# w_ada times silu(c) accumulated by VectorE and summed by matmuls with ones, in place of split matmuls

## What is computed

```
mod = jax.nn.silu(c) @ w_ada + b_ada            # [1, 3072]
shift, scale, gate = jnp.split(mod[:, None, :], 3, axis=-1)
h = rms_norm(x, norm_g) * (1 + scale) + shift
z = h @ w_in
...                                             # MLA attention and MoBA attention on z
return x + gate * y
```

## Time and profile before

| | us |
|---|---|
| median of 3 runs (1778.47 to 1781.76) | 1781.65 |
| profiled execution | 1779.26 |
| its span, first to last instruction | 1777.2 |
| PE busy in the span | 1680.2 |
| VectorE busy | 1063.4 |
| ScalarE busy | 902.1 |
| mean granted TensorE clock | 0.973 |

### The profile page before, as it was taken

One profiled execution on the slowest core, in us unless ns is written; L12 is line 12 of the kernel. 1 busy time (PEld: TensorE's weight loads), 2 busy tenths in 40 slices (PEclk: granted clock), 3 DMA queues, 4 the chain that ended last, 5 costly groups with the idle time before them and its releaser, 6 DMA issues.

```text
span 1777.2 us, 22388 instructions
## 1 busy us (share of the span) xinstructions
PE 1680.2 (95%) x8020; PEld 1366.7 (77%) x8020; DVE 1063.4 (60%) x1761; ACT 902.1 (51%) x1552; POOL 119.5 (7%) x156
## 2 busy tenths in 40 slices
PE   5889889989999999999999999999999999999998
PEld 3667767778888777787778887888878787778886
DVE  4765667557555555566665555665455566765553
ACT  4566636655444454645454444544355644554442
POOL 3010101000000020000200000000030000200000
PEclk7999989999999999999999999999999999999999
DMA  8675226424555582353655555655673353646552
GB/s 272 216 242 157 81 77 213 137 72 156 189 188 191 153 216 92 113 166 102 212 178 189 187 180 155 195 184 190 189 180 107 111 167 112 202 157 191 186 192 80
DMA packets 155050, 292.25 MB, mean 164 GB/s; under 512 B 10182, under 2 KB 23284, under 8 KB 154940
## 3 DMA queue, kind: packets, MB, share of 16 engines
q1 hardware_dynamic: 149312, 276.60, 48.4%
q0 software_dynamic: 4512, 11.24, 2.8%
q10 hardware_dynamic: 1116, 2.99, 0.5%
HBM read 289.72 MB, written 1.06 MB: 164 GB/s over the span
## 4 chain that ended last, share of the span: by engine, by line
PE 78%; DVE 8%; ACT 5%; DMA 4%; issue 3%; POOL 1%; SPq 0%; DVEq 0%; POOLq 0%; ACTq 0%
PE pb L421 73%; PE pb L425 4%; ACT wh L787 2%; DMA raw<-in_w_in 2%; DVE wl L1279 2%; DMA raw<-in_w_ada 1%; POOL st L1986 1%; ACT pb L787 1%; DVE dg L1273 1%; ACT p L787 1%; DVE ti L1276 0%; ACT xt_h L787 0%; DMA ring<-in_b_gate 0%; DVE h L1276 0%; DVE xt_l L1276 0%
## 5 line engine op out<-in xcount | busy, mean ns | idle before, releaser
L1279 DVE TENSOR_TENSOR wl<-raw,wh 128x1024 fp32r<-128x1024 f32 (+1 forms) x532 | 632.5, 1219 | 384.9 <-ACT wh L787 380.6
L787 ACT ACTIVATE wh<-raw 128x1024 fp32r<-128x1024 f32 (+1 forms) x532 | 544.3, 1050 | 273.0 <-PE pb L421 240.9
L421 PE MATMUL pb<-wh,xt_h 128*128 128x512 f32 (+2 forms) x1536 | 596.9, 389 | 2.0 <-issue 1.3
L421 PE MATMUL pb<-wh,xt_l 128*128 128x512 f32 (+2 forms) x1536 | 588.0, 383 | 11.0 <-DVE xt_l L1276 11.0
L421 PE MATMUL pb<-wl,xt_h 128*128 128x512 f32 (+2 forms) x1536 | 587.7, 383 | 5.0 <-DVE wl L1279 4.8
L421 PEld LDWEIGHTS pb<-wh,xt_l 128*128 128x128 f32 x1536 | 293.1, 191 | 70.6 <-DVE xt_l L1276 16.1
L421 PEld LDWEIGHTS pb<-wl,xt_h 128*128 128x128 f32 x1536 | 293.7, 191 | 59.0 <-DVE wl L1279 8.0
L421 PEld LDWEIGHTS pb<-wh,xt_h 128*128 128x128 f32 x1536 | 294.0, 191 | 58.3 <-issue 6.7
L421 PE MATMUL pb<-wh,big_h 128*128 128x512 f32 x352 | 140.2, 398 | 0.0
L421 PE MATMUL pb<-wh,big_l 128*128 128x512 f32 x352 | 139.6, 396 | 0.0
L421 PE MATMUL pb<-wl,big_h 128*128 128x512 f32 x352 | 139.5, 396 | 0.0
(11 more groups left out here) (212 smaller groups left out, 1598.8 us busy)
## 6 DMA issues: line engine op xcount, KB each, us to landing
raw<-in_ffn_w_gu SPq DMA_DIRECT2D x176, 512.0 KB, 4.6
raw<-in_w_in SPq DMA_DIRECT2D x148, 512.0 KB, 4.4
raw<-in_ffn_w_down SPq DMA_DIRECT2D x88, 512.0 KB, 4.2
raw<-in_w_ada SPq DMA_DIRECT2D x48, 512.0 KB, 5.6
raw<-in_w_out SPq DMA_DIRECT2D x32, 512.0 KB, 3.6
raw<-in_w_branch SPq DMA_DIRECT2D x24, 512.0 KB, 3.6
raw<-in_w_in SPq DMA_DIRECT2D x8, 416.0 KB, 4.0
G<-in_na_rpb POOLq DMA_DIRECT2D x32, 96.0 KB, 8.7
```

Of the source, the lines that this page charges most:

```text
L421: return e.matmul(o, a, b, start=start, stop=stop)
L787: return e.activation(o, a, func, **kw)
L1279: return e.tensor_tensor(o, a, b, op)
```

## The change

- w_ada chunks are no longer split. ACT does nothing on them. When a chunk has landed, DVE multiplies its two k-rows with silu(c), per partition, and adds them up in an accumulator `acc` (two buffers of 128 x 512, one for each tile in turn): two instructions for each chunk (`weigh`), each waiting for the one before. The raw buffer is free when DVE has read it; wh and wl are only used by the other chunks, which now have a count of their own (i, split_at).
- PE sums the accumulator over partitions: for shift and scale the four one-column matmuls of `turn_row`, now with acc [128, 512] in place of dg [2, 512]; for the gate one matmul with ones for each 512 columns, which sums and spreads at once. DVE adds b_ada, which POOL loads spread over all partitions into `gate`, now in the memory of mk.
- The first four tiles come as (0, 0), (0, 2), (0, 1), (0, 3), and their 16 chunks are all taken ahead of the z gemm. The other tiles have a queue of their own, `later`: in layer 0 (1, 0), (1, 1), (1, 2), (0, 4), (0, 5) over 26 chunk steps, from z to gmoba, and (1, 3) beside the out gemm; in layer 1 (1, 4), (1, 5) over 26.

```diff
@@ pe
-                    for k in range(2):
-                        kx = 2 * kq + k
-                        w.wait_ge(*at("hi", c))
-                        mm(banks[7], cst8[:, kx, 0:128], hi[:, k, :], kx == 0, False)
-                        w.wait_ge(*at("lo", c))
-                        last = mm(banks[7], cst8[:, kx, 1:129], lo[:, k, :], False, kx == 7)
...
         def turn_row(l, j):
+            if j >= 4:
+                return
             b = rot("mod", l, j)
-            w.wait_ge(*at("dgr", l, j))
+            w.wait_ge(*at("acc", l, j, 7))
             for f in range(4):
-                last = mm(b[:, f:f + 1], dg[0:2, f * 128:f * 128 + 128], ones_col, True, True)
+                last = mm(b[:, f:f + 1], acc[ada_no[l, j] % 2][:, f * 128:f * 128 + 128], ones_col, True, True)
...
-            side.add(ada(tiles), 5 * len(tiles))
-            side.over(16)
+            later.add(ada(side_tiles[l, 0]), 5 * len(side_tiles[l, 0]))
+            later.over(26)
...
             for j2 in range(2):
-                o = open_bank(first_bank + j2, ("gcp", l, j2))
-                w.wait_ge(*at("gdg", l, j2))
-                mm(o, ones, dg[:, :], True, True).then_inc(*up("gmm", l, j2))
+                o = open_bank(first_bank + j2, ("gate", l, j2))
+                w.wait_ge(*at("acc", l, 4 + j2, 7))
+                mm(o, ones, acc[ada_no[l, 4 + j2] % 2][:, :], True, True).then_inc(*up("turn", l, 4 + j2))
@@ act
-                        ac_(dg[0:2, :], banks[7][0:2, :]).then_inc(*up("dgr", l, j))
...
-                ac_(gate[:, j2 * 512:j2 * 512 + 512], banks[first_bank + j2]).then_inc(*up("gcp", l, j2))
@@ dve
+        def weigh(c):
+            l, j, kq = plan[c][5]
+            i = ada_no[l, j]
+            for k in range(2):
+                kx = 2 * kq + k
+                v = chunk_view(raw[c % NRAW], c)[:, k, :]
+                weight = stat(8, "c_silu")[:, kx:kx + 1]
+                if kx == 0:
...
+                    ts(acc[i % 2][:, :], v, weight, None, ALU.mult, None).then_inc(*up("acc", l, j, kx))
+                else:
+                    w.wait_ge(*at(f"raw{c % NRAW}", c))
+                    w.wait_ge(*at("acc", l, j, kx - 1))
+                    stt(acc[i % 2][:, :], v, weight, acc[i % 2][:, :], ALU.mult, ALU.add).then_inc(
+                        *up("acc", l, j, kx))
...
-                for j in range(4):
-                    jj = 16 + j2 * 4 + j
-                    last = ts(dg[:, j * 128:j * 128 + 128], ident, mod[:, l, jj:jj + 1], None, ALU.mult, None)
-                last.then_inc(*up("gdg", l, j2))
...
             to_xt(("o", l), 8, XT, 0)
+            for j2 in range(2):
+                v = gate[:, j2 * 512:j2 * 512 + 512]
+                w.wait_ge(*at("turn", l, 4 + j2))
+                w.wait_ge(*at("bgate", l))
+                tt(v, banks[first_bank + j2], v, ALU.add).then_inc(*up("gate", l, j2))
@@ pool
+            b_ = d["b_ada"][l]
+            w.wait_ge(*at("tr", ("mlak", l), 6))
+            e.dma_start(gate, bass.AP(tensor=b_.tensor, offset=b_.offset + 2 * DM, ap=[[0, 128], [1, DM]])).then_inc(
```

More of the change, by code:

```diff
@@ L188, in take @@
         due = []
-        while self.next < len(self.plan) and self.next <= c + AHEAD and self.next - NW < self.freed:
+        while self.next < len(self.plan):
+            split = self.plan[self.next][4]
+            if split is not None and not (split <= c + AHEAD and split - NW < self.freed):
+                break
             due.append(self.next)
             self.next += 1
-        return c, due
+        return due
 def groups(nk, n, head, tail):
@@ L265, in build @@
     pt1 = [sb(f"pt_{i}", [128, 512], F, b1) for i in range(2)]
-    cst8 = sb("cst8", [128, 8, 130], R, b1)
+    acc = [sb(f"acc{i}", [128, 512], F, b1) for i in range(2)]
     rope = sb("rope", [128, 2, 64], F, b1)
@@ L598, in pe @@
         tr(b[:, 0:8], rows[0:8, :]).then_inc(*up("ctr"))
-        first = ada([(0, j) for j in range(4)])
+        first = ada(first_tiles)
         for _ in range(5):
@@ L775, in act @@
         w = Waits(e)
-        side = Side()
+        side, later = Side(), Side()
         stream = Stream(plan)
@@ L948, in act @@
         ac_(stat(8, "c_t"), cols[:, 0:8], ACT.Tanh, scale=0.5).then_inc(*up("ctanh"))
[L949 to L952, removed]
+        stream.lead(16)
+        first = ada(first_tiles)
         for _ in range(5):
@@ L980, in act @@
                     ac_(xt_h[:, c + j, :], xtmp[(c + j) % 2]).then_inc(*up("xh", ("x", l), c + j))
-            dg_read[:] = [("xl", ("x", l), 7)]
-            tiles = [(1, 4), (1, 5)] if l else [(0, 4), (0, 5)] + [(1, j) for j in range(4)]
-            side.add(ada(tiles), 5 * len(tiles))
-            side.over(16)
+            later.add(ada(side_tiles[l, 0]), 5 * len(side_tiles[l, 0]))
+            later.over(26)
             gemm(("z", l), XT, 8, 416, to(lambda t: z0[:, t, :]))
@@ L1058, in act @@
             pair_no[0] += 1
-            first_bank = 2 * ((pair_no[0] - 1) % 2)
+            later.drain()
             side.drain()
-            w.wait_ge(*at("od", "mla", l, 1))
-            for j2 in range(2):
-                w.wait_ge(*at("gmm", l, 1))
-                ac_(gate[:, j2 * 512:j2 * 512 + 512], banks[first_bank + j2]).then_inc(*up("gcp", l, j2))
+            later.add((None for _ in range(4)), 4)
+            later.add(ada(side_tiles[l, 1]), 5 * len(side_tiles[l, 1]))
+            later.over(8)
             to_xt(("o", l), 8, XT, 0)
@@ L1468, in dve @@
         ts(stat(8, "c_silu"), stat(8, "c_s"), 0.5, None, ALU.mult, None).then_inc(*up("csil"))
-        w.wait_ge(*at("chi"))
-        tt(cst8[:, :, 0], stat(8, "c_silu"), cst8[:, :, 1].bitcast(F), ALU.subtract).then_inc(*up("cst8"))
-        first = ada([(0, j) for j in range(4)])
+        w.wait_ge(*at("csil"))
+        first = ada(first_tiles)
         def rows_norm(l):
@@ L1490, in dve @@
         rows_norm(0)
+        for c in stream.lead(6):
+            weigh(c)
         for _ in range(8):
@@ L1679, in dve @@
             pair_no[0] += 1
-            w.wait_ge(*at("mod", l, 5))
-            for j2 in range(2):
-                if j2:
-                    w.wait_ge(*at("gmm", l, 0))
-                for j in range(4):
-                    jj = 16 + j2 * 4 + j
-                    last = ts(dg[:, j * 128:j * 128 + 128], ident, mod[:, l, jj:jj + 1], None, ALU.mult, None)
-                last.then_inc(*up("gdg", l, j2))
+            first_bank = 2 * ((pair_no[0] - 1) % 2)
+            later.drain()
             side.drain()
+            later.add((None for _ in range(4)), 4)
+            later.add(ada(side_tiles[l, 1]), 5 * len(side_tiles[l, 1]))
+            later.over(8)
             for t in range(2):
@@ L2078, in sp @@
         w = Waits(e)
-        for c, (src, kk, n, _) in enumerate(plan):
+        for c, (src, kk, n, _, _, _) in enumerate(plan):
             if c >= NRAW:
-                w.wait_ge(*at("hi", c - NRAW))
-                w.wait_ge(*at("lo", c - NRAW))
+                old = plan[c - NRAW][5]
+                if old:
+                    w.wait_ge(*at("acc", *old[:2], 2 * old[2] + 1))
+                else:
+                    w.wait_ge(*at("hi", c - NRAW))
+                    w.wait_ge(*at("lo", c - NRAW))
             e.dma_start(chunk_view(raw[c % NRAW], c), src).then_inc(*landed(f"raw{c % NRAW}", c))
```

129 lines of the change are left out of this document (76 added, 53 removed).

## The result

The changed kernel takes 1740.0 us (median of 4 runs, 1737.49 to 1740.49), 0.9767 of the time before (95% interval 0.975 to 0.9784). The forecast was 1747 in a range of 1734 to 1762. The profiled execution took 1740.04 us, 39.2 less than before's 1779.26, where the sum said 34.5.

What follows compares the result with a forecast made beforehand. PE was taken to set the pace, VectorE 70% busy beside it. 4.1 + 24.2 - 6 + 4 + 9.2 - 1 = 34.5 us off the profiled 1779.26 gives 1744.8; with 2.4 for the median, 1747 us, range 1734 to 1762.

Steps and rivals of the forecast that it cites:

- Start-up: Before the first x product at 52.44 us: removed copies, splits and matmuls gain 4.1 us, bounds 0 and 6.
- Accumulation: VectorE's new 128x512 instruction: 0.75 us long, starting every 0.78 us, each waiting for the one before.
- Layer 0's stage: First z split to head transposes: 58 us in place of 82.2, set by VectorE and not PE, gain 24.2 us.
- the sign that I had named: In layer 0's projection stage VectorE is busy over 90%; if PE is still the busier one, the prediction is wrong.
- PE's 45 us: PE's work in layer 0's projection stage: its chunks 42.2 us, two turns and the c transposes 3.
- Attention: Layer 0, behind the head transposes: remaining ada chunks on VectorE delay PE, loss 6 us, bounds 1 and 12.
- Gate: Between last pv and out gemm: PE's waits of 2.96 us go, 0.9 lost to bias additions; gain 2 us a layer.
- Layer 1: Its projection stage, 52.1 us before: PE sets it at 43 us, VectorE at 39 stays below; gain 9 us.
- PE's relief in full: Rival: VectorE's waits are filled, layer 0's stage takes 52.4 us, attention loses 1; total 1736 us; chance 0.15.
- The clock: Rival: short pauses hold PE at 1.2 GHz for two thirds of layer 0's stage; total 1755 us; chance 0.2.
- The backlog through attention: Rival: VectorE's backlog costs attention its bound of 12 us and the gate gives nothing; total 1757 us; chance 0.1.
- Costlier accumulations: Rival: each accumulation on the path costs over 1.4 us in place of 0.78, kernel slower than before; chance 0.03.

Runs made afterwards that it cites:

- e1: The changed kernel with the second of each w_ada chunk's two accumulations cut to 8 columns, leaving out most of the sum: 1730.8 us.
- e11: The changed kernel with eight raw buffers in place of six and four buffers each for wh and wl in place of five: 1757.0 us.
- e12: The changed kernel with angle steps moved into the x transform's gaps and tile (1, 2) beside layer 0's out gemm, first chunk behind the gate's additions: 1734.7 us.
- e5: The changed kernel loading only the first k-row of each w_ada chunk from the 17th on, 256 KB in place of 512: 1738.6 us.
- e9: The changed kernel with VectorE's splits of kb's and vb's fourth chunks put ahead of the norms, in both layers: 1739.9 us.
- e7: The changed kernel with VectorE's 19 small angle steps moved from its two norm blocks into the gaps of the x transform: 1736.1 us.
- e8: The changed kernel with one side tile of each layer, (0, 5) and (1, 5), moved beside the MLA attention: 1741.8 us.
- e10: The changed kernel with side tile (1, 2) moved from layer 0's steps z to gmoba to beside its out gemm: 1740.7 us.

## Why the prediction held

**Start-up** (4.1, measured 4.2): right, by its own steps; e1 shows that VectorE sets it.

**Accumulation** at 0.75 us and 0.78 from start to start: right. Two of them:

```profile
65.95 1.53 DVE L1284 SCALAR_TENSOR_TENSOR acc<-raw,st,acc 128x512 f32<-128x512 f32 x2
```

The Trainium skill (VectorE: DVE Perf Modes, The DRAIN you can't avoid) would have the wait on the one before free; the trace again speaks mildly against it, at 0.03 us behind the end.

**Layer 0's stage** (58, measured 57.3): right number, half the reason, so its closeness is luck in part. VectorE's sum was right: vb's last split ends 54.6 us behind the stage's start (forecast 53.7), and the head transposes come 2.7 behind it (forecast 2.75). But VectorE was 86% busy, not over 90%, and by the sign that I had named, PE not the busier one, it is a tie (49.80 and 49.55). A shorter list moves the split and not the stage (e1, and e11 with its 52.1). The step that failed is PE's 45 us. PE alone takes 48.6 in e12 without a wait, and most of the 3.6 more are the z chunks: 12.2 us in place of 9.1, because PE begins them at the lower clock (their products start 0.35 us apart up to 64.8 us, 0.19 from there on). The changed kernel, at the stage's start and around the pause:

```profile
59.57:63.80 4.23, 3.84 (x10) 3.31 (x11) 4.20 (x6) 2.33 (x3) 0.00 (x0) 0.50 0.43 133
98.00:104.80 6.80, 4.41 (x10) 3.47 (x11) 6.56 (x13) 1.65 (x2) 0.00 (x0) 0.50 0.39 119
```

Here PE's own line is 11.5 us for z, 35.5 for the 144 products of 512 columns (forecast 33.1; 2.4 of it lost at 0.50 behind the pause), 3.1 for the rest and the pause of 7.0: 57.2 us. I had named the pause and its place, but added only 1.5 us for it, behind VectorE's sum, and nothing in PE's. So two limits lay within a microsecond: VectorE's list, and PE's work with the pause that the norm block makes and the clock behind it. Edits on one alone gained at most 1.7 us in the stage (e1, e5, e9, e11); what shortened the list and with it the pause gained 4 to 5 us (e7, e8, e10; pauses 2.3 to 2.6).

**Attention** (-6, measured -8.4): mechanism right, size short. Heads to first mask is 7.94 us (5.45 before), so 2.5 in place of the 3.5 charged. Nor does PE stand still there, as I expected: it is busy for 7.48 of the 7.94, and its waits come behind the first mask. The rest, 5.9 us, falls in the stretch with the four chunks behind it (6.2 us of accumulations), where I charged 2.5, with the argument that PE had 8 us of slack. ScalarE's waits for the mask's sums, from the head transposes to mq, in the changed kernel and before:

```profile
ACT pb L802 <- DVE st L1290: 14.6, 6, 5.0
...
ACT pb L787 <- DVE st L1282: 5.9, 6, 2.9
```

None of PE, VectorE and ScalarE waits for a load in that stretch. The granted clock over it is 0.90 against 0.92 before, so at most some 2 of the microseconds are the clock's. That such slack is none, e8 shows too.

**Gate** (2 a layer, measured 3.9 and 3.8): the 2.96 us of waits were read rightly; the lower clock beside them was not priced, nor were the new waits of 1.75. The 0.9 us for the bias additions did not appear (out to x 27.7 before, 27.8 after).

**Layer 1** (9.1, measured 11.6): PE's 43 us were 40.5. The last two z chunks took 6.95 us, as charged (4.6 and 2.3), the third at the lower clock. What was not there is the 0.9 us ahead of PE's first product (0.1 measured), the 1 us of waiting (0.55, already within the 6.95), 0.4 of the c transposes and 0.2 of the twelve other chunks; VectorE, 35.0 of 40.5 us busy, did not bind.

**The rivals.** PE's relief in full: no, the stage is 57.3 and attention -8.4; that the total came near its 1736 is the gate and layer 1. The clock: it stands at 0.50 at the stage's start and again from within the long pause, so PE lost 4.8 us to it (z 11.5 for 9.1, the products of 512 columns 35.5 for 33.1), a mechanism that the sum left out. But the stage's mean is 0.90: 11 of 57.3 us at the lower level, not two thirds, and none of it after a run of short pauses. The backlog through attention: its condition came closer than its price, -8.4 in layer 0 against the bound of 12, and the gate gave 7.7 where that rival had nothing. Costlier accumulations: no.

**The sum.** 34.5 against 39.2 in the profile: the gate and layer 1 gave 3.6 and 2.5 us more than forecast, the two attentions 3.3 less, so the errors partly cancel.

**Median.** 2.4 of the 7 us between 1747 and 1740.0 is the distance of the profiled run from the median before, which the changed kernel doesn't have.

## What to carry to other kernels

When work is taken from the busiest engine, work out its new sum and that of the next one, and add to each the pauses that the removed work had been filling: here both came to 57 us, and cutting VectorE's work alone did not move the stage. Idle time of an engine that works in a chain with others is not room for side work; idle gaps where it waits a known 0.5 us for another engine, as in the x transform, are (19 steps there cost 0.1 us). Price a wait of PE with the granted clock around it, not with its length alone.

## What the runs showed of the hardware

From the end of a wait of 1.90 us, over 7.6 us with a second wait of 1.06, PE's granted clock was 0.55 on average; with three waits of 0.47, 0.74 and 0.54 it stood at 1.00 in the same place. A shorter pause did not cost less of the clock: behind one of 7.04 us PE worked 4.4 us at 0.50, behind one of 3.58 us (e11) 9.19 us, busy throughout. The Trainium skill (TensorE: Matmul & The Clock Gate, A second HAM failure mode: psum-queue depth-cycling) tells of pauses between groups of matmuls that make the clock swing; the gate agrees; the stage, with one long pause, shows one fall only.
